# State space stage: first blocks' matrices evicted ahead of the sines, waits per bank, last outputs in another bank

## What is computed

```python
u = h @ w_in
...
bu_r = jnp.einsum("tbgc,gpc->tbgp", u_chunk, bb_r)
bu_i = jnp.einsum("tbgc,gpc->tbgp", u_chunk, bb_i)
pw_r, pw_i, s_r, s_i = lax.associative_scan(_ssm_combine, (a_r, a_i, bu_r, bu_i), axis=0)
x_r = s_r + pw_r * x_r0 - pw_i * x_i0
x_i = s_i + pw_r * x_i0 + pw_i * x_r0
y = (jnp.einsum("tbgp,gcp->tbgc", x_r, cr) - jnp.einsum("tbgp,gcp->tbgc", x_i, ci))
...
y = y + d_skip.astype(f32) * u.astype(f32)
g = jax.nn.gelu(y).astype(h.dtype)
val, gate = jnp.split(g @ w_glu, 2, axis=-1)
return val * jax.nn.sigmoid(gate)
```

## Time and profile before

| | us |
|---|---|
| median of three runs | 2930.0 (2928.68 to 2933.07) |
| the profiled execution | 2930.7 |
| its span, first to last instruction | 2928.9 |
| TensorE's mean granted clock | 0.974 |
| busy in the span: PE, DVE, POOL, ACT | 2613.1, 1938.6, 1676.3, 826.5 |
| u's last slab ends, the stage begins | about 1643 |
| last outputs (L1024) end, the GLU begins | about 1747 |

### The profile page before, as it was taken

The page is one execution under the profiler, slowest core; times in us unless marked ns, Lnnn a source line. Parts: engine busy times, 40 slices in busy tenths (PEclk is TensorE's granted clock), DMA queues, the critical chain, the costliest instruction groups (busy, mean ns, idle before and its releaser), DMA issues.

```text
span 2928.9 us, 32483 instructions
## 1 busy us (share of the span) xinstructions
PE 2613.1 (89%) x9868; PEld 1216.2 (42%) x9868; DVE 1938.6 (66%) x3952; ACT 826.5 (28%) x1802; POOL 1676.3 (57%) x1024
## 2 busy tenths in 40 slices
PE   7989888888878888877878999999999998999999
PEld 3554333333333333333333684444444445444444
DVE  8847777777777777777877683566336696566423
ACT  3423222222222222222234462222112146222101
POOL 5544444444444444444535876777776651677776
PEclk9999999999999999999998979999999999999999
DMA  4259999999999999999971323333322420233322
GB/s 141 68 203 421 421 421 419 414 415 413 417 415 410 411 409 419 416 415 415 409 322 62 108 67 99 94 100 103 116 96 83 130 65 8 80 101 103 119 99 81
DMA packets 133260, 696.06 MB, mean 238 GB/s; under 512 B 30051, under 2 KB 31372, under 8 KB 67212
## 3 DMA queue, kind: packets, MB, share of 16 engines
q0 software_dynamic: 73728, 536.90, 44.5%
q1 hardware_dynamic: 59404, 157.61, 16.5%
HBM read 688.16 MB, written 7.88 MB: 238 GB/s over the span
## 4 chain that ended last, share of the span: by engine, by line
PE 33%; DMA 25%; POOLq 16%; DVE 12%; issue 8%; ACT 3%; DVEq 2%; POOL 2%; ACTq 0%; SPq 0%
DMA R<-expert_uv_dram,idx 25%; PE bank L588 20%; PE bank L816 8%; POOLq L2730 8%; POOLq L2728 7%; DVE R L2158 3%; POOL R L2755 1%; DVE Z L2180 1%; DVE xt L2443 1%; ACT Z L1434 1%; DVE R L1894 1%; PE bank L1167 1%; PE bank L985 1%; DVE R L2170 0%; DVE ci L2104 0%
## 5 line engine op out<-in xcount | busy, mean ns | idle before, releaser
L816 PE MATMUL bank<-R,Z 128*128 128x512 f32 x2048 | 966.3, 616 | 234.3 <-ACT Z L1434 229.3
L2755 POOL DMA_INDIRECT R<-expert_uv_dram,idx x512 | 598.5, 1169 | 720.8 <-PE bank L816 668.8
L588 PE MATMUL bank<-R 128*128 128x512 f16 (+1 forms) x3936 | 864.6, 381 | 6.5 <-DVE R L1876 2.5
L2158 DVE SCALAR_TENSOR_TENSOR R<-R 128x1024 f32<-128x1024 f32 x512 | 623.1, 1222 | 204.2 <-DMA R<-expert_uv_dram,idx 203.2
L816 PEld LDWEIGHTS bank<-R,Z 128*128 128x128 f32 x2048 | 379.6, 194 | 805.5 <-issue 414.7
L2727 POOL TENSOR_TENSOR R<-wring,beat 128x1024 f16<-128x1024 f32 (+2 forms) x219 | 446.7, 2040 | 390.2 <-PE bank L588 345.1
L588 PEld LDWEIGHTS bank<-R 128*128 128x128 f16 (+1 forms) x3936 | 383.7, 98 | 482.1 <-issue 21.2
L2729 POOL TENSOR_TENSOR R<-wring,R 128x1024 bf16<-128x1024 f32 (+2 forms) x219 | 509.7, 2328 | 31.9 <-issue 0.3
L1434 ACT ACTIVATE Z<-consts,R 128x128 f32<-128x128 f32 x512 | 177.7, 394 | 321.3 <-DVE R L2170 319.4
L588 PE MATMUL bank<-Z,R 128*128 128x512 f16 x1104 | 239.9, 379 | 1.5 <-POOLq L2730 1.5
L1427 ACT ACTIVATE R<-R 128x2 f32<-128x2 f32 x256 | 52.1, 203 | 608.4 <-DVEq L2160 608.1
(11 more groups left out here) (369 smaller groups left out, 2513.3 us busy)
## 6 DMA issues: line engine op xcount, KB each, us to landing
wring<-up_dram SPq DMA_DIRECT2D x88, 512.0 KB, 3.5
wring<-down_dram SPq DMA_DIRECT2D x32, 704.0 KB, 4.1
wring<-ple_dram SPq DMA_DIRECT2D x16, 640.0 KB, 3.9
wring<-w_in_dram SPq DMA_DIRECT2D x18, 512.0 KB, 3.5
R<-expert_uv_dram,idx POOLq DMA_INDIRECT x512, 12.3
wring<-glu_dram SPq DMA_DIRECT2D x16, 512.0 KB, 4.4
Z<-w_q_dram SPq DMA_DIRECT2D x11, 512.0 KB, 8.3
wring<-ple_a_dram SPq DMA_DIRECT2D x8, 640.0 KB, 6.0
```

Of the source, the lines that this page charges most:

```text
L588: mm = pe.matmul(bank[:, :], low(w) if i else w, low(v) if j else v, start=(start and c == 0 and p == 0), stop=(stop and c == n - 1 and p ...
L816: mm = pe.matmul(banks[2 * par + c][:, :], diag[:, k % 4, :], pairs[:, slot, 1, c * SEQ:(c + 1) * SEQ], start=(k == 0), stop=(k == TOPK - 1))
L2158: dot = ve.scalar_tensor_tensor(pairs[:, slot, 0, :], pairs[:, slot, 0, :], 1.0, ntok[:, T, :], ALU.mult, ALU.mult, accum_out=act[:, par, ...
L2755: po.indirect_dma_start(pairs[:, slot, :, :].rearrange("p a b -> p (a b)"), None, A["expert_uv"], bass.IndirectOffsetOnAxis(idx[:, n % 2, ...
```

## The change

Four edits. PE no longer waits for the last eviction of u before the stage, but before each bank's first use for that bank's own eviction (tiles 4, 5 and 6 of u for banks 0, 1 and 2). ACT evicts the matrices of block 0 before `sines(0)`, and those of block 1 before `sines(1)` and `swap_states(0)`. The last block's outputs go to bank 2 (`last_bank`) and wait for the last eviction of bank 2 (`h_ev`) in place of the copy of block 6's outputs (`yo_ev`). The GLU's slab 2, whose bank is 2 as well, gets a wait for the copy of the last outputs.

```diff
--- before.py
+++ after.py
@@ -311,6 +311,7 @@
         glu_spare = parts_of(R, 2048, 2, WSLOT - 3 * P)
         v_bank, swap_bank, ph_bank, y_bank = banks[4], banks[5], banks[6], banks[7]
         GELU_BANKS = (ph_bank, v_bank)
+        last_bank = banks[2]
         swapped, turns = xt[:, 0, :], xt[:, 1, :]
         bigP, bigN, bigM = [view(R, 7168 + 1024 * i, GROUPS, 2 * CH) for i in range(3)]
         whole_turns = psum[:, 4 * SEQ:6 * SEQ].rearrange("p (g i) -> p g i", i=2 * CH)
@@ -964,12 +965,16 @@
                     for half in range(2):
                         if n:
                             pe.wait_ge(te_ev, 2 * n - 1 + half)
+                        else:
+                            pe.wait_ge(evac_done, used(TILE0["ssm_in"] + KT - 4 + half))
                         for g in range(4):
                             mm = pe.transpose(banks[half][:, g * P:(g + 1) * P], row(gmat[:, n % 2, half * 4 + g, :, :]),
                                               ident)
                         mm.then_inc(bt_mm, 1)
                     if n:
                         pe.wait_ge(h_ev, n)
+                    else:
+                        pe.wait_ge(evac_done, used(TILE0["ssm_in"] + KT - 2))
                     for g in range(GT):
                         mm = pe.matmul(banks[2][:, g * GC:(g + 1) * GC], row(gmat[:, n % 2, g, :, :]),
                                        Cm[:, n * GT + g, :], start=True, stop=True)
@@ -1013,19 +1018,18 @@
                                            xpad[:, g, 0:NCH], start=False, stop=True)
                         mm.then_inc(y_mm, 1)
                         return
-                    pe.wait_ge(yo_ev, n)
-                    pe.matmul(y_bank[:, :], zeros, zeros[:, 0:1].broadcast_to([1, SEQ]), start=True, stop=False)
+                    pe.wait_ge(h_ev, KT)
+                    pe.matmul(last_bank[:, :], zeros, zeros[:, 0:1].broadcast_to([1, SEQ]), start=True, stop=False)
                     for g in range(GT):
-                        pe.matmul(y_bank[:, g * NCH:(g + 1) * NCH], Tg[:, n % 2, g, :], uall[:, n, g * NCH:(g + 1) * NCH],
+                        pe.matmul(last_bank[:, g * NCH:(g + 1) * NCH], Tg[:, n % 2, g, :], uall[:, n, g * NCH:(g + 1) * NCH],
                                   start=False, stop=False)
                     pe.wait_ge(e_ready, n + 1)
                     pe.wait_ge(x_ready, n + 1)
                     for g in range(GT):
-                        mm = pe.matmul(y_bank[:, g * NCH:(g + 1) * NCH], row(emat[:, n % 2, g, :, :]),
+                        mm = pe.matmul(last_bank[:, g * NCH:(g + 1) * NCH], row(emat[:, n % 2, g, :, :]),
                                        xpad[:, g, 0:NCH], start=False, stop=(g == GT - 1))
                     mm.then_inc(y_mm, 1)
 
-                pe.wait_ge(evac_done, used(TILE0["ssm_in"] + KT - 1))
                 input_matrices(0)
                 chunk_inputs(0)
                 output_matrices(0)
@@ -1050,6 +1054,8 @@
 
                 for i in range(3):
                     pe.wait_ge(split_done, used(s0 + i))
+                    if i == 2 and stage("ssm"):
+                        pe.wait_ge(yo_ev, KT)
                     glu_product(i, n=KT - 3, ready=x_split if i == 0 else None, base=base, stop=False, first_of_slab=False)
                 for i in range(3):
                     glu_product(i, n=2, ready=x_split if i == 0 else None, base=base + KT - 3, start=False, stop=False,
@@ -1684,7 +1690,7 @@
                     ac.wait_ge(y_mm, n + 1)
                     if n >= 2:
                         ac.wait_ge(y_stored, 16 * (n - 1))
-                    ac.activation(ysb[:, n % 2, :], y_bank[:, :], ACT.Copy).then_inc(yo_ev, 1)
+                    ac.activation(ysb[:, n % 2, :], (y_bank if n < KT - 1 else last_bank)[:, :], ACT.Copy).then_inc(yo_ev, 1)
 
                 def gelus(n):
 
@@ -1697,16 +1703,16 @@
                     ac.drain()
                     ac.activation(XO[:, n, 0, :], bank[:, :], ACT.Copy).then_inc(x_gelu, 1)
 
+                input_matrices(0)
                 sines(0)
                 decays(0)
-                input_matrices(0)
                 swap_inputs(0)
                 output_matrices(0)
                 cosines(1)
+                input_matrices(1)
                 sines(1)
                 swap_states(0)
                 decays(1)
-                input_matrices(1)
                 output_matrices(1)
                 for n in range(KT):
                     if n + 1 < KT:
```

## The result

| | us |
|---|---|
| before, median of 8 runs | 2929.82 (2928.62 to 2933.07) |
| after, median of 8 runs | 2939.12 (2935.97 to 2941.88) |
| ratio, 95% interval | 1.0023 (1.0013 to 1.0034) |
| profiled execution of after, its span, clock | 2939.3, 2937.5, 0.970 |
| profiled execution of before, its span, clock | 2930.7, 2928.9, 0.974 |

The change made the kernel some 9 us slower, 0.2 to 0.3%. The forecast was 2931.2, and the median lies 2.1 us above its range too (2926.0 to 2937.0); by the ratio, 1.0023 times 2930.0, it is 2936.7, at the range's edge. The measured time is near the rival "Slower" (2936.3), which had 0.18. The executions of one kernel here spread by 4 to 6 us. What sets them apart isn't shown, since only one of each set was profiled: a profile is one course among several.

The account below looks back on a forecast made before the run. PE was late in the opening, then POOL and DVE together paced the loops. Opening -0.5, middle clock 0 and tail clock +1.7 us summed to +1.2 on 2930.0, giving 2931.2 us, range 2926.0 to 2937.0.

Parts of the forecast that it names:

- the rival "Slower": Opening: PE waits for POOL's block-2 matrix, its clock falls, later low stretches add cost; +6.3 us, 2936.3 us, chance 0.18.
- Waits per bank: Start of the stage: PE waits for POOL's matrix instead of the last eviction of u; gain 0.4 us at most.
- The evictions: Opening: block 0's makes `chunk_inputs(0)` 0.8 us earlier, block 1's comes 3.4 us earlier; second scan 3.1 us earlier, up to 6.
- Opening, -0.5 us: Opening and loops: POOL limits the gain, four loops shorten from 11.57 to 11.4 us; -0.5 us, between 0 and -3.1.
- The clock in the middle: Middle of the stage: PE's half-clock stretches lie elsewhere but cost the same; 0 us, between -4.9 and +3.4.
- The reading that the clock rose only in L985 or GLU matmuls: Opening, within the slower rival: the clock stays low through transposes, 16-column products and `outputs(0)`, which take 12.4 us.
- my upper bound of 3.4: Middle of the stage: at worst one more half-clock stretch of 6.8 us, costing +3.4 us.
- The lower bound: Middle of the stage: at best the low stretches vanish, winning the 4.9 us of them taken to lie on the path.
- Last outputs in bank 2: End of the stage: the GLU's first matmul comes 2.1 us earlier but then waits for its tiles; worth 0.
- The clock in the tail: Last outputs and first GLU tiles: more gaps make PE's clock rise later; +1.7 us, between 0 and +3.4.

Follow-up runs that it names:

- `block0_only`: The kernel before with only block 0's matrices evicted by ACT ahead of `sines(0)`; median 2931.61 us, ratio 1.0001.
- the two halves: The kernel before with only the waits per bank and ACT's new order, median 2933.8 us; and with only the last outputs' new bank, median 2933.59 us.
- `opening_only`: The changed kernel with the last outputs back in their old bank (7) and no new GLU wait; median 2933.8 us, ratio 1.0012.
- `thin_all`: The changed kernel with added matmuls on constants, 16 columns each, wherever PE waits or is thinly used; 2962.0 us, ratio 1.0104.
- `fill_all`: The changed kernel with added matmuls on constants, 128 columns each, wherever PE waits or is thinly used; median 2938.94 us, ratio 1.0026.
- `fill_open`: The changed kernel with 20 added matmuls of 128 columns on constants in PE's wait for block 2's matrix; median 2933.15 us, ratio 1.0017.

## Why the prediction was wrong

*Waits per bank, at most 0.4 us.* Right: 0.

*The evictions.* Right in kind, and larger than forecast: L1653's counterpart ran at 1651.7 (forecast 1656 to 1657), and the second scan came 7.6 us early, 6.1 in the stage (forecast 3.1, up to 6). Some 3 us of that no edit aims at: before's low stretch from 1646.8 to 1653.6 didn't come, so `chunk_inputs(0)` took 1.98 in place of 3.68 us and `output_matrices(0)` 2.00 in place of 3.51. The wait before L985 went, and PE waited for POOL before `input_matrices(2)`.

*Opening, -0.5 us.* Wrong in sign. POOL's waits were the right place to look: its `out_of_states` started at 1672.16 and 1695.64, against 1673.09 and 1696.22, but A is 1.5 us earlier, so in the stage POOL is 0.6 and 0.9 us later. The working assumed that DVE would be early in four loops and L2551 would fall between POOL's operations. DVE was early for one scan; for the third it waited 3.86 us for the product of a PE that had been at half clock.

*The clock in the middle, 0 (-4.9 to +3.4).* This is the step that failed. The mechanism stood in the text as the rival "Slower": PE waits for POOL's matrix, its clock falls, and transposes, 16-column products and `outputs(0)` run at half speed. They did: 11.9 us (1659.97 to 1671.87, forecast 12.4). (The reading that the clock rose only in L985 or GLU matmuls wasn't exact: in before it also rose at 1721.9, in the `chunk_inputs` that began at 1721.34.) But it was priced at one more stretch of 6.8 us and given 0.18. The trace has two of 17.1 us in place of the 10.2 and 6.8: the first turns a second scan that is 6 us early (7.6 less the 1.5 of A) into a third that is 2.9 us late (1679.04 against 1677.66, with A's 1.5), and the second puts PE behind DVE again before the last scan. A to B is 5.2 us longer, above my upper bound of 3.4, which was half of one more stretch of 6.8 us, the shorter of the two in the middle. The trace before has one of 17.1 us, which ends 44 us ahead of the stage:

```profile
1581.90:1599.00 17.10, 11.48 (x41) 0.50 0.00 1
```

There PE is busy for 11.48 us of it. An upper bound on the clock's cost ought to have come from that one. It would be a bound and no forecast: this one in `block0_only` cost nothing up to C (122.71 us from A).

```profile
1734.40:1751.50 17.10, 15.04 (x61) 0.50 0.21 61
```

The lower bound was wrong too. It put 4.9 us of the low stretches of before on the path, yet DVE waited there for nothing over 0.3 us up to the last scan, as the prediction itself read from its rows, so there was next to nothing to win.

*Last outputs in bank 2, worth 0.* Right from B to C in the traces, 35.13 against 35.14 us. By the medians the bank costs 3 us alone and 5 on top of the opening, and the traces account for less than that (see Open).

*The clock in the tail, +1.7 (0 to +3.4).* Right for the last bank alone (+1.76). With the opening it was +3.4, of which 1.4 to 1.6 are DVE's tiles, which I had taken as unmoved within 1 us. This term too was mis-sized: 3.4 us where 1.7 was taken, at its upper bound.

*Outside the stage.* A stretch of 3.4 us where the GLU ends was not in the sum. Half of it, 1.7 us, is all that the clock can cost there by my estimate, and it shows in ten of the fourteen traces, `block0_only` among them, so it isn't tied to one edit.

Open: the two halves cost 3.3 and 3.1 us by the medians and the whole 9. In the traces of the long course the opening has the whole stage loss by itself (A to C 131.98), and three of eleven executions of `opening_only` took that long, against seventeen of nineteen of the change at 2935.9 or more. Why the new bank makes the long course the usual one isn't shown. No version here beats the kernel before.

## What to carry to other kernels

Before an engine is made early, see what it will wait for next: here each edit of the opening alone was free, and the loss began when PE overtook POOL and an idle 2.5 us was followed by 17 us at half clock. Where a change brings such a wait, let the upper bound of the clock's cost come from the longest low stretch anywhere in the trace, and then ask which engine would wait for PE in it: the one of 17.1 us in `block0_only` cost nothing up to C. And compare kernels between fixed starts inside the stage, as A to C here, since executions of one and the same kernel lay up to 11.5 us apart (`opening_only`).

## What the runs showed of the hardware

- With added matmuls of 16 columns PE was busy 20.50 of 20.50 us and stayed at 1.2 GHz (`thin_all`); with 128 columns in the same places it ran at 2.4 GHz in that stretch (`fill_all`). In `thin_all` the clock fell with no idle of PE in the 7 us ahead of the fall.
- After a wait of 3.09 us followed by `output_matrices` (128 columns) the clock was low for 3.4 us in the trace before; after a shorter wait, 2.51 us, followed by transposes and products of 16 and 64 columns, for 17.1 us.
- Low stretches of the same length cost different amounts: from A to C, after with two and a part of a third took 132.11 us, `block0_only` with one of 13.7 and one of 17.1 took 122.71, and before with none over 13.6 took 123.44.
- Of `fill_open` nine executions took 2930.7 to 2935.6 us and two 2941; what sets them apart isn't shown.
- DVE's subtraction with both inputs in SBUF took 1.33 us in before and 2.49 in after at the end of the stage, beside POOL's operations.
